# A two-model forward pass on one core: 512-column split products issued as two 256-column halves

## The chip, the cores and the metric

The kernel runs on one core of a Trainium2 chip. The metric is the device time of one execution in microseconds; the time given for a kernel is the median of its runs. TensorE does the matrix products, VectorE (DVE in the profile), ScalarE (ACT) and GpSimd (POOL) the rest, and SyncE (SP) issues the transfers.

## The reference, cut to what matters

Two small models run one after the other on 256 tokens of width 1024, all in float32. The first has a retention layer, a per-layer embedding, a layer of native sparse attention (NSA) and a second per-layer embedding. The second puts 16 meta tokens ahead of the 256, mixes a gated delta rule with forgetting attention, and ends with a SwiGLU block of width 2816. Nearly all of the arithmetic is in products of the token rows with weight matrices:

```
proj = rmsnorm(h, g_norm) @ w_in                # retention: 1024 x 6144
y = (silu(gate) * o) @ w_out                    # retention: 2048 x 1024
gate = sigmoid(rmsnorm(h, g) @ w_gate)          # embedding, twice: 1024 x 1024
proj = rmsnorm(h, g_kv) @ w_kv                  # 1024 x 3072
proj = rmsnorm(h, g_norm) @ w_in                # NSA: 1024 x 4144
y = (silu(gate) * o) @ w_out                    # NSA: 2048 x 1024
proj = u @ w_in[l]; ... @ w_out[l]              # second model: 1024 x 3600, 1024 x 1024
h = h + (silu(x @ w_gate) * (x @ w_up)) @ w_down  # 1024 x 2816 twice, 2816 x 1024
```

## The kernel before

**Split products.** A float32 product is made of three one-pass products. Each operand is kept as a high part (its value rounded to the one-pass type `F32R`) and a low part (what the rounding left). `parts3` (line 762) adds high by high, low by high and high by low into one PSUM region; the low by low term is left out. ScalarE rounds a weight (line 1621, `high_parts<-ring`), VectorE subtracts (line 2060, `ring_parts<-ring,high_parts`), each in halves of 1024 columns.

**Units.** The weights come in units of 128 x 2048 numbers (1 MB each) through a ring of four buffers `ring`; the high parts go to three buffers `high`. SyncE issues a unit when TensorE has begun the unit three before it and so has left the one in that buffer (`units_used`, which the first matmul of a unit raises). The splitting engines run a fixed number of units ahead of TensorE. A matmul's wait for its unit is on `units_low`.

**Two shapes of product.** Units of kind A hold 8 tiles (contraction) by 256 output channels; there the weight tile of 128 x 128 is the stationary operand and the 256 tokens (272 in the second model) are the moving one, so a pass has 256 or 272 columns (`project_a`, line 803 on; `project_a_pair`; `channels_input`). Units of kind B hold 4 tiles by 512 channels; there the 128 x 128 tile of tokens is stationary and the weights move, so a pass has 512 columns and fills a PSUM bank. All the products of 512 columns are of kind B, and their functions are `project_b` (line 818 on), `retention_output` (1006), `first_rows_output` (1216), `mix_output` (1411), `rows_input` (1447) and the down projection (1597 and 1603). A unit of kind B gives 8 split products, 24 matmuls; a unit of kind A gives 16, 48 matmuls. The compression layer of NSA (`first_layer`) has products of its own, not through `parts3`: the stationary operand is a 128 x 124 tile that holds both parts, the moving one 256 columns of a weight unit.

**The 488 products of 512 columns, in order of time**: retention values and gate (`rv`, `rg`, 128 products), retention output (`ro`, 64), first embedding gate (`pg`, 32), the row half of the shared key and value projection (`kvB`, 32), NSA output (`no`, 64), second embedding gate (`pg`, 32), the `gz` gate rows (16) and the mixer output (`mo`, 32), the down projection (`dn`, 88). Three passes each make 1464 matmuls. From the second embedding to `mo`, the token tiles stand in rows of 272 with an offset of 16; elsewhere they stand in rows of 256.

**Order.** Each engine has its own instruction list, written out by hand in the order of the network; between projections TensorE transposes token tiles (`turn`, line 841), does the attention products and the delta rule. `narrow` (line 757) is a list of small products that `parts3` puts between its passes; it is filled only ahead of products of 256 columns (`nq`, `ng`) and is used up by them.

Of the kernel before, what the change touches and what calls it, by code (L numbers as in the profile page):

```python
# [351 lines left out]
def two_models_kernel(nc, x, meta, weights, side, params, tabs, ret_tabs, p_t, gains, out):  # L352
    ctx = ExitStack()
    with ctx:
# [10 lines left out]
        def as_r(ap):  # L365

            return bass.AP(tensor=one_pass[ap.tensor.name], offset=ap.offset, ap=ap.ap)
# [303 lines left out]
        def odd_blocks(ap, lv):  # L671

            return ap.rearrange("p (b two m) -> p b two m", two=2, m=LEVELS[lv])[:, :, 1, :]

        def level_rows(lv, c):
            return chunk_part(c, G1, 1024, 1) if lv else z_rows(c)
# [79 lines left out]
        def _(pe):  # L756
            narrow = []

            def mm(out, lhsT, rhs, first, last):
                return pe.matmul(out, lhsT, rhs, start=first, stop=last, skip_group_check=True)  # L760

            def parts3(product, out, lhsT, rhs, first, last):

                product(out, as_r(lhsT[0]), as_r(rhs[0]), first, False)
                if narrow:
                    narrow.pop(0)()
                product(out, as_r(lhsT[1]), as_r(rhs[0]), False, False)
                if narrow:
                    narrow.pop(0)()
                return product(out, as_r(lhsT[0]), as_r(rhs[1]), False, last)  # L770

            def next_unit(k):

                u = begun[0]
                begun[0] += 1
                if u == 0:
                    pass
                elif IS_SPLIT[u]:
                    pe.wait_ge(sem("units_low"), 2 * SPLITS[u] - 1)
                else:  # L780
                    pe.wait_ge(sem(f"unit_in{u % RING}"), 16 * (u // RING + 1))
                first = [u > 0]

                def product(*args):
                    ins = mm(*args)
                    if first[0]:
                        ins.then_inc(sem("units_used"), 1)
                    first[0] = False
                    return ins

                low = ring[:, u % RING * UNIT:(u % RING + 1) * UNIT].rearrange("p (k c) -> p k c", k=k)
                hi = high[:, u % HIGH * UNIT:(u % HIGH + 1) * UNIT].rearrange("p (k c) -> p k c", k=k)
                second = [u > 0 and IS_SPLIT[u]]

                def w(i, c):
                    if second[0] and 2 * i >= k:
                        pe.wait_ge(sem("units_low"), 2 * SPLITS[u])
                        second[0] = False
                    return hi[:, i, c], low[:, i, c]

                return w, product

            def project_a(keys, src, c0, n):

                w, product = next_unit(KD)
                for f in range(2):
                    key = keys[f * (len(keys) - 1)]
                    base = f * n if len(keys) == 1 else 0
                    if f == 0 or len(keys) == 2:
                        bank = main.open(pe, key)  # L810
                    for k in range(KD):
                        x_k = src(k, c0, n)
                        ins = parts3(product, bank[:, base:base + n], w(k, slice(f * P, (f + 1) * P)), x_k,
                                     k == 0, k == KD - 1)
                    if f == 1 or len(keys) == 2:
                        main.full(ins, key)

            def project_b(keys, src, rows, kt, ready=None, started=None):

                banks = [main.at(key) if started and n == 0 else main.open(pe, key) for n, key in enumerate(keys)]  # L820
                for k0 in range(0, kt, 4):
                    if ready:
                        ready(k0)
                    w, product = started if started and k0 == 0 else next_unit(4)
                    for n, bank in enumerate(banks):
                        if started and k0 + n == 0:
                            continue
                        c0, m = rows[n]
                        for k in range(4):
                            x_k = src(k0 + k, c0, m)  # L830
                            ins = parts3(product, bank[0:m, :], x_k, w(k, slice(0, 512)), k0 + k == 0,
                                         k0 + k == kt - 1)
                        if k0 + 4 == kt:
                            main.full(ins, keys[n])
# [69 lines left out]
            def x_src(k, c0, n):  # L904
                tile_ready("x", k)
                return kt_cols(xT, k, c0, n), kt_cols(xT2, k, c0, n)

            def tokens_src(k, c0, n):
                tile_ready("x", k)
                return kt_cols(xT, k, c0, n, T), kt_cols(xT2, k, c0, n, T)  # L910
# [24 lines left out]
            w, product = next_unit(KD)  # L935
            for f in range(4):
                pe.wait_ge(sem(piece_low(f)), 1)
                for half in range(2):
                    for k in (2 * f, 2 * f + 1):
                        ins = parts3(product, bank[:, half * T:(half + 1) * T], w(k, slice(half * P, (half + 1) * P)),  # L940
                                     tokens_src(k, 0, T), half == 0 and k == 0, k == KD - 1)
# [8 lines left out]
            for kt in range(KD):  # L950
                ins = pe.transpose(bank[:, kt * M:(kt + 1) * M], R[0:M, R3 + kt * P:R3 + (kt + 1) * P], ident[0:M, 0:M])
# [3 lines left out]
            def qk_tile(which, hd, half, c0, n):  # L955
                return kt_cols(R, which * 8 + hd * 2 + half, c0, n, T, R1)

            pe.wait_ge(sem("rotated"), 8)
            for hd in range(RH):
# [3 lines left out]
                for half in range(2):  # L963
                    ins = mm(bank[:, T:T + P], qk_tile(1, hd, half, P, P), qk_tile(0, hd, half, P, P),
                             half == 0, half == 1)
# [284 lines left out]
            for k in range(KD):  # L1250
                w_k = gates_high[:, k * 16:(k + 1) * 16], side_sb[:, SIDE_G2 + k * 16:SIDE_G2 + (k + 1) * 16]
                ins = parts3(mm, bank[0:16, 0:TM], w_k, x_src(k, 0, TM), k == 0, k == KD - 1)
# [7 lines left out]
            def mat(buf, base, c, hd):  # L1260
                n = CHUNKS[c][1]
                return buf[0:n, base + C_OFF[c] + hd * n:base + C_OFF[c] + (hd + 1) * n]

            def of_head(rows, c, hd):
                n = CHUNKS[c][1]
                return rows[:, hd * n:(hd + 1) * n]

            def chunk_rows(base, c, hd):

                buf, b0 = base  # L1270
                return buf[0:CHUNKS[c][1], b0 + c * 512 + hd * P:b0 + c * 512 + (hd + 1) * P]
# [180 lines left out]
            for kind, *key in mixer_order():  # L1452
# [35 lines left out]
                elif kind == "Lz":  # L1488
                    lv, c = key
# [9 lines left out]
                    for hd in range(GH):  # L1499
                        ins = mm(bank[0:n, hd * n // 2:(hd + 1) * n // 2].rearrange("p (b m) -> p b m", m=LEVELS[lv]),  # L1500
                                 of_head(level_rows(lv, c), c, hd), odd_blocks(mat(PTb, C_ALL, c, hd), lv), True, True)
                    aux.full(ins, ("z", lv, c))
                    if lv > 1:
                        bank = aux.open(pe, ("x", lv, c))
                        for hd in range(GH):
                            ins = pe.transpose(bank[0:n, hd * n:(hd + 1) * n], mat(PTb, C_ALL, c, hd), ident[0:n, 0:n])  # L1506
                        aux.full(ins, ("x", lv, c))
                elif kind == "Lx":
                    lv, c = key
# [6 lines left out]
                    for hd in range(GH):  # L1516
                        half = slice(hd * n // 2, (hd + 1) * n // 2)
                        ins = mm(bank[0:n, half], mat(PTb, 0, c, hd), z[:, half], True, True)
                    aux.full(ins, ("y", lv, c))
                elif kind == "W":  # L1520
                    c = key[0]
# [3 lines left out]
                    for hd in range(GH):  # L1525
                        ins = mm(bank[:, hd * P:(hd + 1) * P], chunk_rows(RK, c, hd), mat(PTb, C_ALL, c, hd), True, True)
                    aux.full(ins, ("gw", c))
                elif kind == "Vn":
                    c = key[0]
# [8 lines left out]
                    for hd in range(GH):  # L1538
                        o = bank[0:n, hd * P:(hd + 1) * P]
                        ins = mm(o, mat(PTb, C_ALL, c, hd), chunk_rows(RV, c, hd), True, c == 0)  # L1540
                        if c:
                            w0 = (c - 1) * 512 + hd * P
                            ins = mm(o, nw[:, w0:w0 + P], R[:, state + hd * P:state + (hd + 1) * P], False, True)
                    aux.full(ins, ("vn", c))
                else:
                    c = key[0]
                    t0, n = CHUNKS[c]
                    wait_read(pe, aux, ("vn", c))
                    if c:
                        pe.wait_ge(sem("q_scaled"), c)  # L1550
                        bank = aux.open(pe, ("go", c))
                        for hd in range(GH):
# [3 lines left out]
                            ins = mm(o, R[:, k0:k0 + P], R[:, v_new + hd * P:v_new + (hd + 1) * P], False, True)  # L1556
                        aux.full(ins, ("go", c))
                    if c < 2:
                        wait_read(pe, aux, ("kt", c))
                        bank = aux.open(pe, ("st", c))  # L1560
                        for hd in range(GH):
                            ins = mm(bank[:, hd * P:(hd + 1) * P], chunk_rows(KDEC, c, hd),
                                     R[0:n, v_new + hd * P:v_new + (hd + 1) * P], True, True)
# [19 lines left out]
            def hidden_src(k, t):  # L1583
                return tuple(hidden(k, part)[:, t * P:(t + 1) * P] for part in range(2))

            banks = {}
            for c in range(2):
                for k0 in range(0, 20, 4):
# [3 lines left out]
                    w, product = next_unit(4)  # L1592
# [6 lines left out]
            w, product = next_unit(2)  # L1599
            for t in range(TT):  # L1600
                for c in range(2):
                    for k in range(2):
                        ins = parts3(product, banks[c, t], hidden_src(20 + k, t), w(k, slice(c * 512, (c + 1) * 512)),
                                     False, k == 1)
# [1258 lines left out]
```

## Time and profile before

| | |
|---|---|
| median of 3 runs | 957.28 us (954.9 to 960.26) |
| the profiled execution: its time, its span | 956.0 us, 954.2 us |
| TensorE matmul busy | 941.8 us, 99% of the span, 6366 matmuls |
| TensorE weight loads busy | 843.8 us, 88%, 6366 loads |
| VectorE, ScalarE, GpSimd busy | 66%, 50%, 13% |
| granted TensorE clock | 0.999 of full speed |
| weight transfers | 135 of 1024 KB, mean 158 GB/s in all |

Matmuls overlap in the pipe: a record of a 512-column pass is about 0.39 us long, but the next pass starts about 0.23 us after it. So the busy time of TensorE says only that it was never without work; how fast it works is read from the distance between the starts of successive matmuls, called the pitch here. A window of the trace gives the number of matmuls in it and with that the pitch. The window counts each matmul that overlaps it, also those that started before it and were still in the pipe: 0.28 us of 256-column records, or 0.39 us of 512-column records.

### The profile page before, as it was taken

The page shows a single profiled execution, that of the slowest core. Times are in us where ns is not written, and L with a number is a line of the kernel's source. Part 1 is how long each engine was busy: PE and PEld are TensorE (multiplying, and loading weights), DVE is VectorE, ACT ScalarE, POOL GpSimd, SP SyncE. Part 2 cuts the span into 40 slices and gives each one's busy share as a digit, 9 for nine tenths or more (in the row PEclk, how much of TensorE's full clock was granted, in tenths as well). Part 3 has the DMA queues.
Part 4 walks back from the last instruction along what each step waited for, and adds up shares of the span by engine and source line. Part 5 has one row for each costly group of instructions (what it writes and reads, how often), then busy time and mean ns, then how long its engine had stood idle before and what let it go on. Part 6 is the DMA issues. An engine that isn't in the chain of part 4 may idle for free.

```text
span 954.2 us, 15895 instructions
## 1 busy us (share of the span) xinstructions
PE 941.8 (99%) x6366; PEld 843.8 (88%) x6366; DVE 632.9 (66%) x930; ACT 478.9 (50%) x843; POOL 122.0 (13%) x128
## 2 busy tenths in 40 slices
PE   9999999999999999999999999999999999999997
PEld 8988778878998999998888789999998899999885
DVE  5974467557884766678874477988554677676543
ACT  6334446455654554466653566664335554444432
POOL 1000032000320000101410004212320111111001
PEclk9999999999999999999999999999999999999999
DMA  8735445555555763332025553522101455565551
GB/s 327 291 138 180 158 147 177 177 177 177 177 194 214 289 231 133 131 136 89 1 88 178 175 177 134 177 89 89 46 1 45 167 190 196 184 213 179 191 206 45
DMA packets 23516, 150.55 MB, mean 158 GB/s; under 512 B 3564, under 2 KB 3848, under 8 KB 6168
## 3 DMA queue, kind: packets, MB, share of 16 engines
q1 hardware_dynamic: 23104, 149.39, 44.8%
q8 instruction: 51, 0.84, 0.3%
q10 hardware_dynamic: 344, 0.18, 0.1%
q14 instruction: 17, 0.14, 0.1%
HBM read 148.50 MB, written 1.05 MB: 157 GB/s over the span
## 4 chain that ended last, share of the span: by engine, by line
PE 86%; DVE 7%; ACT 3%; issue 1%; DMA 1%; POOL 0%; SPq 0%; ACTq 0%; POOLq 0%; DVEq 0%
PE psum L760 83%; DVE ring_parts L2060 3%; PE psum L841 1%; DVE R L2385 1%; ACT high_parts L1621 1%; ACT R L1806 1%; PE psum L1174 1%; DMA h<-in_x 1%; DMA ring<-in_weights 1%; DVE R L2337 1%; PE psum L1506 1%; DVE PTb_parts L2356 0%; ACT tmp L1659 0%; ACT R L1628 0%; PE psum L1357 0%
## 5 line engine op out<-in xcount | busy, mean ns | idle before, releaser
L2060 DVE TENSOR_TENSOR ring_parts<-ring,high_parts 128x1024 fp32r<-128x1024 f32 (+1 forms) x272 | 333.3, 1264 | 146.7 <-ACT high_parts L1621 145.3
L1621 ACT CAST high_parts<-ring 128x1024 fp32r<-128x1024 f32 x268 | 268.2, 1050 | 187.0 <-PE psum L760 149.2
L760 PE MATMUL psum<-xT_parts,high_parts 128*128 128x256 f32 (+1 forms) x1024 | 227.5, 284 | 1.5 <-issue 0.6
L760 PE MATMUL psum<-xT_parts,ring_parts 128*128 128x256 f32 (+1 forms) x704 | 200.1, 284 | 0.0
L760 PEld LDWEIGHTS psum<-xT_parts,high_parts 128*128 128x128 f32 x1024 | 172.3, 188 | 3.0 <-issue 1.2
L760 PE MATMUL psum<-high_parts,R_parts 128*128 128x512 f32 (+1 forms) x528 | 164.9, 386 | 0.0
L760 PE MATMUL psum<-R_parts,high_parts 128*128 128x256 f32 x832 | 156.0, 277 | 0.0
L760 PE MATMUL psum<-high_parts,xT_parts 128*128 128x512 f32 x480 | 154.2, 397 | 0.0
L760 PEld LDWEIGHTS psum<-xT_parts,ring_parts 128*128 128x128 f32 x704 | 132.9, 189 | 0.1
L760 PEld LDWEIGHTS psum<-R_parts,high_parts 128*128 128x128 f32 x832 | 130.5, 188 | 0.1
L760 PEld LDWEIGHTS psum<-high_parts,R_parts 128*128 128x128 f32 (+1 forms) x528 | 98.7, 188 | 20.5
L760 PEld LDWEIGHTS psum<-high_parts,xT_parts 128*128 128x128 f32 x480 | 89.4, 188 | 20.9 <-issue 1.9
L760 PE MATMUL psum<-ring_parts,xT_parts 128*128 128x512 f32 x256 | 100.6, 393 | 0.0
L760 PE MATMUL psum<-ring_parts,R_parts 128*128 128x512 f32 (+1 forms) x264 | 99.3, 381 | 0.0
L760 PE MATMUL psum<-R_parts,ring_parts 128*128 128x256 f32 x352 | 97.2, 276 | 0.0
L760 PE MATMUL psum<-PTb_parts,high_parts 128*128 128x256 f32 x256 | 73.8, 288 | 0.0
L760 PEld LDWEIGHTS psum<-R_parts,ring_parts 128*128 128x128 f32 x352 | 66.1, 188 | 0.0
L760 PEld LDWEIGHTS psum<-ring_parts,R_parts 128*128 128x128 f32 (+1 forms) x264 | 49.6, 188 | 9.6
L760 PEld LDWEIGHTS psum<-ring_parts,xT_parts 128*128 128x128 f32 x256 | 48.1, 188 | 10.6
L760 PEld LDWEIGHTS psum<-PTb_parts,high_parts 128*128 128x128 f32 x256 | 48.2, 188 | 0.0
L760 PE MATMUL psum<-R 128*128 128x128 f32 (+3 forms) x248 | 47.1, 324 | 0.6 <-DVE R_parts L2572 0.6
L2737 POOL TENSOR_TENSOR R<-R,small 128x1024 f32<-128x1024 f32 x12 | 22.8, 1899 | 194.7 <-DVE small L2332 194.7
(354 smaller groups left out, 1144.4 us busy)
## 6 DMA issues: line engine op xcount, KB each, us to landing
ring<-in_weights SPq DMA_DIRECT2D x135, 1024.0 KB, 4.9
h<-in_x SPq DMA_DIRECT2D x4, 256.0 KB, 4.6
ring<-in_weights SPq DMA_DIRECT2D x4, 256.0 KB, 6.2
ring<-in_weights SPq DMA_DIRECT2D x2, 512.0 KB, 7.6
G<-in_gains SPq DMA_DIRECT2D x2, 512.0 KB, 7.7
out<-xn SPq DMA_DIRECT2D x2, 512.0 KB, 2.6
R<-in_ret_tabs SPq DMA_DIRECT2D x1, 768.0 KB, 13.6
tab<-in_tabs SPq DMA_DIRECT2D x1, 663.5 KB, 5.9
```

Source lines behind the costliest of these rows:

```text
L760: return pe.matmul(out, lhsT, rhs, start=first, stop=last, skip_group_check=True)
L841: ins = pe.transpose(bank[:, k * T + t * P:k * T + (t + 1) * P], src(2 * f + k, t), ident)
L1174: ins = pe.transpose(bank[:, n * P:(n + 1) * P], R[:, c0:c0 + P], ident)
L1506: ins = pe.transpose(bank[0:n, hd * n:(hd + 1) * n], mat(PTb, C_ALL, c, hd), ident[0:n, 0:n])
L1621: act.copy(as_r(hi), value).then_inc(sem("units_high"), 1)
L1806: ins = act.activation(R[:, c0:c0 + n_keys], bank[:, n * n_keys:(n + 1) * n_keys], ACT.Exp, bias=nmx[:, col:col + 1], accum_out=esum[:, co ...
L2060: return dve.tensor_tensor(as_r(value), value, value_of(hi), ALU.subtract)
L2337: main.free(dve.tensor_tensor(two(R[:, R4 + n * 512:R4 + (n + 1) * 512]), two(bank), token_scale2, ALU.mult), key)
L2385: ins = dve.scalar_tensor_tensor(y, raw[:, j, k:k + TM], param("conv_w_2", 12 * k + j), y, ALU.mult, ALU.add)
L2737: pool.tensor_tensor(p, p, spread(esc[:, i * 8:i * 8 + 2 * nh], 1024 // (2 * nh)), ALU.mult).then_inc(sem("nsa_p"), 1)
```

## The change

In `parts3`, a product whose output is two-dimensional and 512 columns wide is no longer three passes of 512 columns. It is three passes over the left 256 columns of the bank, then three over the right 256, in the order high by high, low by high, high by low, with the same stationary tiles. Only the first pass of the left half carries the start flag of the bank. Outputs of other widths, and the three-dimensional output of the NSA values (line 1199), go the old way. The new branch doesn't call `narrow`.

```
             def parts3(product, out, lhsT, rhs, first, last):
 
+                if len(out.shape) == 2 and out.shape[1] == 512:
+                    for c in (slice(0, 256), slice(256, 512)):
+                        product(out[:, c], as_r(lhsT[0]), as_r(rhs[0][:, c]), first and c.start == 0, False)
+                        product(out[:, c], as_r(lhsT[1]), as_r(rhs[0][:, c]), False, False)
+                        ins = product(out[:, c], as_r(lhsT[0]), as_r(rhs[1][:, c]), False, last)
+                    return ins
                 product(out, as_r(lhsT[0]), as_r(rhs[0]), first, False)
```

## Rows read from the trace of the kernel before

**Rows 1.** The page: busy time and instructions of each engine, and their chain.
```profile
PE 941.8 (99%) x6366; PEld 843.8 (88%) x6366; DVE 632.9 (66%) x930; ACT 478.9 (50%) x843; POOL 122.0 (13%) x128
...
PE 86%; DVE 7%; ACT 3%; issue 1%; DMA 1%; POOL 0%; SPq 0%; ACTq 0%; POOLq 0%; DVEq 0%
```
**Rows 2.** Groups: out<-moving,stationary, shapes, count, busy us, mean ns, idle before.
```profile
L760 PE MATMUL psum<-high_parts,R_parts 128*128 128x512 f32 x496 | 157.2, 393 | 0.0
L760 PE MATMUL psum<-high_parts,xT_parts 128*128 128x512 f32 x480 | 154.2, 397 | 0.0
L760 PE MATMUL psum<-ring_parts,xT_parts 128*128 128x512 f32 x256 | 100.6, 393 | 0.0
L760 PE MATMUL psum<-ring_parts,R_parts 128*128 128x512 f32 x232 | 91.5, 394 | 0.0
...
L760 PEld LDWEIGHTS psum<-R_parts,high_parts 128*128 128x128 f32 x832 | 130.5, 188 | 0.1
L760 PEld LDWEIGHTS psum<-high_parts,R_parts 128*128 128x128 f32 x496 | 92.8, 188 | 20.5
```
**Rows 3.** Windows of 512-column passes: stretch; length, PE and PEld busy (count), clock.
```profile
284.00:304.00 20.00, 20.00 (x89) 16.43 (x88) 1.00 0.59 206
...
493.50:533.00 39.50, 39.50 (x171) 32.01 (x171) 1.00 0.51 171
548.00:560.00 12.00, 12.00 (x53) 9.76 (x52) 1.00 0.57 199
...
888.00:946.00 58.00, 58.00 (x255) 47.61 (x254) 1.00 0.42 145
```
**Rows 4.** Windows of passes of 256 columns, the same columns.
```profile
24.00:51.00 27.00, 27.00 (x232) 27.00 (x231) 1.00 0.73 261
...
250.00:282.00 32.00, 32.00 (x285) 32.00 (x284) 1.00 0.64 224
...
314.00:319.00 5.00, 5.00 (x45) 5.00 (x44) 1.00 0.92 382
...
362.00:364.00 2.00, 2.00 (x19) 2.00 (x18) 1.00 0.91 360
404.00:409.00 5.00, 5.00 (x46) 5.00 (x45) 1.00 0.52 170
...
435.00:440.00 5.00, 5.00 (x47) 5.00 (x46) 1.00 0.57 192
...
609.00:612.00 3.00, 3.00 (x28) 3.00 (x27) 1.00 0.62 164
...
778.00:886.00 108.00, 108.00 (x955) 108.00 (x954) 1.00 0.58 202
```
**Rows 5.** Timeline of the NSA values and first NSA output products.
```profile
489.29 0.28 PE L760 MATMUL psum<-PTb_parts,R_parts 128*128 128x256 f32 x1
...
490.37 0.28 PE L760 MATMUL psum<-PTb_parts,R_parts 128*128 128x256 f32 x1
490.49 0.63 PE L760 MATMUL psum<-high_parts,R_parts 128*128 128x512 f32 x2
490.96 0.40 PE L760 MATMUL psum<-ring_parts,R_parts 128*128 128x512 f32 x1
491.19 0.63 PE L760 MATMUL psum<-high_parts,R_parts 128*128 128x512 f32 x2
```
**Rows 6.** Timeline of the compression layer, first and last of 16 passes.
```profile
360.02 0.28 PE L760 MATMUL psum<-high_parts,xn_parts 128*124 128x256 f32 x1
...
361.90 0.28 PE L760 MATMUL psum<-xT_parts,high_parts 128*128 128x256 f32 x1
```
**Rows 7.** The chain in order of time: eight transposes of 128 columns.
```profile
231.77 0.87 PE psum L841 x8
```
**Rows 8.** The page's groups: the two engines that split the weights.
```profile
L2060 DVE TENSOR_TENSOR ring_parts<-ring,high_parts 128x1024 fp32r<-128x1024 f32 (+1 forms) x272 | 333.3, 1264 | 146.7 <-ACT high_parts L1621 145.3
L1621 ACT CAST high_parts<-ring 128x1024 fp32r<-128x1024 f32 x268 | 268.2, 1050 | 187.0 <-PE psum L760 149.2
```
**Rows 9.** TensorE's waits for the split: us in total, times, longest.
```profile
PE psum L760 <- DVE ring_parts L2060: 0.5, 2, 0.3
```

## The prediction, made before the changed kernel ran

> **What bounds the kernel now.** I read the page first, for who is busy and who ends the chain, then the groups with their shapes kept apart, then windows of single stretches, and last the timeline where a window was too coarse. The page [rows 1] is to show that TensorE is never without work: 99% busy, and 86% of the chain that ends last. Whatever changes the number of nanoseconds that a matmul takes from the stream changes the end of the kernel by the same amount, as long as nothing else becomes the bound. The groups [rows 2] are to show two things. The four groups of 512 columns hold 496 + 480 + 256 + 232 = 1464 passes, which is 3 for each of 488 products, so all of them can be costed. And none of them stood idle before, so in these stages TensorE waits for nothing: neither for a weight unit nor for a bank.
>
> The mean of 393 to 397 ns in those groups is the length of a record in the pipe, not what a pass costs. The cost is the pitch, from windows. A window counts the passes that overlap it; for 512 columns that is 0.39 / 0.23 = 1.7 passes too many, for 256 columns 0.28 / 0.115 = 2.4.
>
> 512 columns [rows 3]: 20 / (89 - 1.7) = 229.1 ns, 58 / (255 - 1.7) = 229.0; in the NSA output 39.5 / (171 - 1.7) = 233.3; with token rows of 272, 12 / (53 - 1.7) = 233.9, where one pass more or less in the count is 2% (so I take 232).
>
> 256 columns [rows 4]: 32 / (285 - 2.4) = 113.2 ns and 108 / (955 - 2.4) = 113.4; but 27 / (232 - 2.4) = 117.6, 5 / (45 - 2.4) = 117.4 and 3 / (28 - 2.4) = 117.2. A third level is in the timeline of the NSA values [rows 5]: nine passes from 489.29 to 490.37, 120.0 ns each; the 512-column product that follows takes 490.49 to 491.19, 233.3 ns a pass.
>
> So the same instruction runs at two or three levels: 113.3 (call it the even level), 117.7, and 120. The stretch at 24 us and the one at 778 us are the same kind of stream, a weight tile stationary and 256 tokens moving; I found nothing in the shapes that sets the level. It seems to be taken at the start of a stretch and kept. That is what this forecast hangs on, because 2 x 113.3 = 226.7 is less than 229.0, and 2 x 117.7 = 235.4 and 2 x 120 = 240 are more.
>
> **The change, part by part.**
>
> Removed: 1464 passes of 512 columns. Today they cost, by product of three: 344 products in rows of 256 at 3 x 229.0 = 687.0 ns; 64 of the NSA output at 3 x 233.3 = 700 ns; 80 in rows of 272 (second embedding gate 32, gz 16, mixer output 32) at 3 x 232 = 696 ns. The sum is 236.3 + 44.8 + 55.7 = 336.8 us, or 690.2 ns a product.
>
> Added: 2928 passes of 256 columns, each with its load of a 128 x 128 stationary tile; the third and the fourth pass load the same tile, and it is loaded twice (in the compression layer [rows 6] two passes in a row have the same tile and still take 1.88 us / 16 = 117.5 ns each). The trace has no pass of exactly this kind: 128 token columns stationary, 256 columns of a weight unit moving. The nearest rows bound it. Below: 113.3 ns, the even level [rows 4], made of the same column counts with the operands exchanged. Above: 120 ns [rows 5], tokens moving and V stationary, the slowest steady stream of this shape. Between them lies the compression layer [rows 6], nearest in its moving operand (the same buffers, 256 columns), 117.5 ns with an odd tile of 124 columns. A product becomes 6 x 113.3 = 680, 6 x 117.7 = 706 or 6 x 120 = 720 ns.
>
> Which value I take, by stage. For the 344 products: of the streams of 256 columns with rows of 256, those at 117.6 or so last 34 us (up to 55 us) and some 20 us in short pieces ([rows 4] has two), while the even ones last from 250 to 283, 778 to 887 and, in pieces, most of 394 to 443 (5 / (46 - 2.4) = 114.7 and 5 / (47 - 2.4) = 112.1 in two of them), so about a fifth of the passes are slow. 0.8 x 680 + 0.2 x 706 = 685 ns, against 687: 344 x -2 = -0.7 us. For the NSA output, the NSA values before it feed it at 120 and today's 512-column passes there keep their extra 6.7 ns each [rows 3, 5]: 720 against 700, 64 x 20 = +1.3 us. For rows of 272, tiles at odd offsets gave 117.2 [rows 4] and 117.5 [rows 6]; 6 x 117.5 = 705 against 696, 80 x 9 = +0.7 us. Sum: +1.3 us.
>
> The bounds of the sum: all at 113.3, 488 x 680 = 331.8 us, -5.0 us; all at 117.7, 344.5 us, +7.7 us; all at 120, 351.4 us, +14.6 us.
>
> The Trainium skill ("TensorE: Matmul & The Clock Gate", section "Back-to-back issue gap") states a fixed part of 2.5 ns in each warm matmul beside its columns, which speaks against halving: 3 more passes are 7.5 ns a product, an estimate of +3.7 us. The rows agree in part: they show no fixed part at all at the even level (113.3 against half of 226 to 229), and a larger one, 5 to 7 ns, at the other two.
>
> What doesn't cost. The order left, then right only moves when the first half is done; the bank is handed over after the last pass as before. The `narrow` list is empty in all 512-column products. The unit's first matmul still raises the signal for the next transfer. Issue: streams of 256 columns already bring a load and a matmul every 113 ns for 108 us on end [rows 4]. Splitting: a kind-B unit lasts 8 x 687 = 5.5 us today and 5.4 to 5.8 us after, while the split takes 2 x 1.26 us of VectorE and 2 x 1.05 us of ScalarE [rows 8]; TensorE waited for it 0.5 us in all [rows 9], and kind-A units of 48 x 113.3 = 5.4 us are fed by the same split. If that cover were gone, a unit would wait as in the chain's 7% of VectorE [rows 1], which lies outside these stages. The four-deep ring sees no other pace.
>
> So nearly nothing is gained or lost: the profiled execution of 956.0 us (span 954.2 and 1.8 around it) goes to 957.3; against the median of 957.28, 1.3 us above that profile, I say 958.6.
>
> **The rivals.**
>
> The slow level everywhere. Each stage starts after transposes or scores and could take 117.7, or 120, and keep it. For it: the slow level followed directly on small products at 24 us, and the nearest moving operand shows 117.5. Against it: four fifths of the passes of 256 columns escape it. Its price is +7.7 us, 965.0; with 120 everywhere 971.9. It decides against the kernel beyond the measurement once the mean pitch of the new passes is over (690.2 + 4.8 / 0.488) / 6 = 116.7 ns. Chance 0.2 for a mean of 116.7 to 118.5, 0.06 for more.
>
> The even level everywhere: the halving evens out the odd nanoseconds of the 512-column passes, NSA output included. For it: after 512-column passes at 229 the 256-column streams at 250 and 778 us settled at 113.3. Against it: rows of 272 never show it. -5.0 us, 952.3. Chance 0.1 for a gain of over 2.5 us.
>
> The load becomes the pace. In 512-column streams the load unit is busy 16.43 of 20 us, in 256-column streams all the time [rows 3, 4], and eight transposes of 128 columns, take 0.87 / 8 = 109 ns each [rows 7], although they have half the columns: if that is the load, it has some 4 ns to spare in a pitch of 113.3. Here the tile loaded comes from the token buffers and twice as often; were it to take 125 ns, a product would be 750 ns and the time 957.28 + 488 x 0.060 = 986. For it: the busy column. Against it: the loads of token tiles under 512-column passes have the same record, 188 ns, as those of weight tiles under 256-column passes, which do keep up [rows 2, 4]. Chance 0.04.
>
> The same section of the Trainium skill gives about 131 ns as the sustained spacing at 512 columns and 81 at 128, by which small passes would be much dearer than half; no row shows such a spacing, the 512-column passes stand at 229.
>
> **How the numbers follow.** 0.6 for the forecast case (-2.5 to +4.5 us: 954.8 to 961.8), 0.1 for the even level, 0.2 and 0.06 for the slow ones, 0.04 for the load. About 0.5%, 4.8 us, is what a measurement of this kernel can tell from no change. The even level reaches 952.5 only in full, so faster gets 0.06, slower 0.28 (0.2 + 0.06, half of the load's chance taken as smaller than its price), same 0.66. The range goes from 953.5, with some of the even level, to 966, which takes in the slow level.
>
> **What would show it.** The page should have 7830 matmuls and as many loads, TensorE 99% busy, the load unit over 95%. Windows in the down projection should hold 113.3 ns a pass (0.6 us less for the whole of it), the NSA output 118 to 120, the second embedding gate 117 to 118. If the first windows of `rv` and `rg` show 117.7, the slow rival is right; a load record longer than 188 ns [rows 2] and a pitch over 120 shows the load. New idle time of TensorE before a 512-column bank's product, with VectorE's split as releaser, would refute the cover.

## The result and the profile after

The changed kernel takes 969.54 us (4 runs, 967.63 to 972.85) against 956.09 us (4 runs, 954.56 to 960.26) of the kernel before: ratio 1.0134, 95% interval 1.0104 to 1.0164. It is slower by 1.3%, where 958.6 us and no measurable change had been forecast. The interval leaves out 1, and both sets of runs stand apart: the fastest of the changed kernel is 7.4 us above the slowest of the kernel before.

The page of the changed kernel, busy time and instructions of each engine, then the chain; they answer to [rows 1].

```profile
PE 956.2 (98%) x7830; PEld 920.6 (95%) x7830; DVE 635.0 (65%) x930; ACT 479.2 (49%) x843; POOL 120.5 (12%) x128
...
PE 87%; DVE 7%; ACT 3%; issue 1%; DMA 1%; POOL 0%; SPq 0%; ACTq 0%; POOLq 0%; DVEq 0%
```

The counts are as forecast, and TensorE is as busy and holds as much of the chain as before. Two waits of TensorE are longer than in the first trace of the kernel before, and neither is the change's: at the start, ahead of anything that was changed, it waits 3.5 us in all for the transfer of the tokens (`h<-in_x`) instead of 0.8, and once 1.4 us for VectorE in the second model. The second trace of the kernel before has 2.0 us and 1.4 us for the same two. What changed is the pitch. Windows of the changed kernel (stretch; length, PE busy and count, PEld busy and count, granted clock), which answer to [rows 3] and [rows 4]:

```profile
24.00:51.00 27.00, 27.00 (x241) 27.00 (x240) 1.00 0.74 278
74.00:104.00 30.00, 30.00 (x257) 30.00 (x256) 1.00 0.55 190
114.00:130.00 16.00, 16.00 (x143) 16.00 (x142) 1.00 0.54 193
180.00:205.00 25.00, 25.00 (x215) 25.00 (x214) 1.00 0.47 173
256.00:282.00 26.00, 26.00 (x223) 26.00 (x222) 1.00 0.56 201
...
500.00:538.00 38.00, 38.00 (x325) 38.00 (x324) 1.00 0.52 182
...
640.00:670.00 30.00, 28.55 (x206) 27.09 (x206) 0.83 0.16 53
...
790.00:890.00 100.00, 100.00 (x851) 100.00 (x850) 1.00 0.54 194
908.00:962.00 54.00, 54.00 (x461) 54.00 (x460) 1.00 0.39 137
```

With 2.4 overlapping passes taken off each count, the halves in `rv` (74 to 104) stand at 30 / 254.6 = 117.8 ns, in `ro` (180 to 205) at 117.6, in `no` (500 to 538) at 117.8, in the down projection (908 to 962) at 54 / 458.6 = 117.7; only those of the first `rg` (114 to 130) are near the even level, 113.8. More telling are the streams that the change doesn't touch. The SwiGLU gate and up stream (790 to 890), even at 113.4 before, now takes 100 / 848.6 = 117.8. The key and value stream at 256 went from 113.2 to 117.9. The first stream of all (24 to 51) went the other way, from 117.6 to 113.2, although no instruction ahead of it differs between the two kernels.

The starts of the same matmuls in the two traces, in us:

| stretch | before | after | added |
|---|---|---|---|
| start of the span to 20.9 | 0 to 20.93 | 0 to 22.82 | +1.9 |
| first stream, untouched | 20.93 to 55.42 | 22.82 to 56.04 | -1.3 |
| `rv`, `rg`, `ro`, first `pg`, halves | 55.42 to 237.98 | 56.04 to 241.70 | +3.1 |
| kvA, untouched | 237.98 to 283.08 | 241.70 to 287.96 | +1.2 |
| kvB, halves | 283.08 to 305.06 | 287.96 to 310.57 | +0.6 |
| compression, queries, scores, untouched | 305.06 to 493.44 | 310.57 to 497.86 | -1.1 |
| `no`, second `pg`, halves | 493.44 to 567.17 | 497.86 to 572.43 | +0.8 |
| second model up to the mixer's end, with `gz` | 567.17 to 740.01 | 572.43 to 750.67 | +5.4 |
| `mo`, halves | 740.01 to 765.80 | 750.67 to 776.97 | +0.5 |
| SwiGLU gate and up, untouched | 765.80 to 887.03 | 776.97 to 902.38 | +4.2 |
| down projection, halves | 887.03 to the end | 902.38 to the end | +1.7 |

The halves added 6.8 us in this trace (a little more with the 16 `gz` products, which lie in the row of the second model), and the SwiGLU stream 4.2. The -1.3 of the first stream can't be the change's, since it runs ahead of the first changed instruction. The +1.2 of kvA is not in every execution: matched in the same way, the second trace of the changed kernel (below) has 0.0 for the first stream, +0.1 for kvA, +7.3 for the halves and again +4.2 for SwiGLU. So what the change did to a stream that it doesn't touch, in both traces, is the 4.2 us of SwiGLU.

The 5.4 us in the second model are nearly all TensorE's clock: the window from 640 to 670 has a granted clock of 0.83, which is about 10 us at the lower level of 1.2 GHz; the engine was busy 28.55 of 30 us there, between streams, with many small products. The four executions of the changed kernel differ in it: two took 967.6 and 967.8 us and two 971.2 and 972.9, and the clock over the span was 0.996 and 0.999 in the first two, 0.994 and 0.993 in the others. It is no effect of the change: a second trace of the kernel before (below) has such a dip at 638 us, the kernel with halves in the down projection only (below), whose instructions are those of the kernel before up to 887 us, has two, at 635 and 652 us, and of 66 later executions of the kernel before 29 had a clock of 0.994 or less. The difference is there without the dips: the changed kernel's execution at 0.999 took 967.8 us, and the 23 of the kernel before at 0.999 took 953.7 to 957.2. The two faster ones are 11.6 and 11.8 us above the profiled execution of the kernel before; the table without its row of 5.4 gives 11.6.

### The profile page after: what moved, and what is told of

Read it like the earlier page. It is cut to its first block, busy times and chain, and to the rows that moved or that the text cites. A ratio compares the mean times of both kernels' runs of the same rounds, so it can differ in the third digit from the quotient of the medians.

```text
span 971.2 us, 18823 instructions
## 1 busy us (share of the span) xinstructions
PE 956.2 (98%) x7830; PEld 920.6 (95%) x7830; DVE 635.0 (65%) x930; ACT 479.2 (49%) x843; POOL 120.5 (12%) x128
## 4 chain that ended last, share of the span: by engine, by line
PE 87%; DVE 7%; ACT 3%; issue 1%; DMA 1%; POOL 0%; SPq 0%; ACTq 0%; POOLq 0%; DVEq 0%
PE psum L760 84%; DVE ring_parts L2066 3%; PE psum L847 1%; DVE R L2391 1%; ACT R L1812 1%; DMA h<-in_x 1%; PE psum L1180 1%; ACT high_parts L1627 1%; DVE R L2343 1%; PE psum L1512 0%; DVE PTb_parts L2362 0%; ACT tmp L1665 0%; ACT R L1634 0%; PE psum L1363 0%; DVE PTb L2538 0%
## 5 line engine op out<-in xcount | busy, mean ns | idle before, releaser
L760 PE MATMUL psum<-high_parts,R_parts 128*128 128x256 f32 (+1 forms) x1024 | 190.1, 280 | 0.0
L760 PE MATMUL psum<-high_parts,xT_parts 128*128 128x256 f32 x960 | 178.3, 282 | 0.0
L760 PE MATMUL psum<-R_parts,high_parts 128*128 128x256 f32 x832 | 160.6, 281 | 0.0
L760 PEld LDWEIGHTS psum<-high_parts,R_parts 128*128 128x128 f32 (+1 forms) x1024 | 159.6, 187 | 0.0
L760 PEld LDWEIGHTS psum<-high_parts,xT_parts 128*128 128x128 f32 x960 | 148.7, 188 | 2.1 <-issue 1.9
L760 PE MATMUL psum<-ring_parts,xT_parts 128*128 128x256 f32 x512 | 142.8, 279 | 0.0
L760 PE MATMUL psum<-ring_parts,R_parts 128*128 128x256 f32 (+1 forms) x496 | 137.3, 279 | 0.0
L760 PEld LDWEIGHTS psum<-ring_parts,xT_parts 128*128 128x128 f32 x512 | 96.2, 188 | 0.0
L760 PEld LDWEIGHTS psum<-ring_parts,R_parts 128*128 128x128 f32 (+1 forms) x496 | 93.1, 188 | 0.0
```

## The experiments

All of them are told by the level of the streams, 113.3 (even) or 117.8 (slow) for 256 columns, 229.0 or 233.3 for 512.

**The two kernels again.** No edit.

> The kernel before, unchanged, for a second trace. Theory P (the level of a stream, 113.3 or 117.8 ns a pass, is fixed by the program: by the instructions ahead of it): the same streams are even and slow as in the first trace, 24 to 51 us slow, 250 to 282 and 778 to 886 even, and the time is 954 to 958. Rival R (the level is drawn anew in each execution): at least one of these three streams stands at the other level, and the SwiGLU stream alone moves the time by 954 x 4.4 ns = 4.2 us when it does.

959.52 us. Windows, which answer to [rows 4] at 24, 250 and 778 us:

```profile
26.00:53.00 27.00, 27.00 (x232) 27.00 (x231) 1.00 0.72 267
250.00:282.00 32.00, 32.00 (x285) 32.00 (x284) 1.00 0.58 201
790.00:880.00 90.00, 90.00 (x797) 90.00 (x796) 1.00 0.57 197
```

The same counts as in the first trace: slow, even, even (90 / 794.6 = 113.3). Every long stream of the second trace stands at the level that it had in the first, as theory P has it. Two traces are few, though. The kernel with halves in the down projection only (below) has the same instructions up to 887 us, and in its trace the first stream came out even. Its window, to be compared with the first one above:

```profile
26.00:53.00 27.00, 27.00 (x241) 1.00 0.78 278
```

> The changed kernel, unchanged, for a second trace. Theory P: the first stream (25 to 53 us) even, the streams of rv, rg 0, ro, kvA and kvB, no, the SwiGLU gate and up products and dn slow at 117.8, as in the first trace; 967 to 969 without, up to 973 with a stretch of TensorE at 1.2 GHz. Rival R: the list of slow streams differs from the first trace's, and the time lies anywhere from 957 to 969. If the two stretches at 1.2 GHz around 643 and 656 us are the change's own, they are there again; if they are chance, they aren't.

972.74 us, windows of the second trace of the changed kernel:

```profile
24.00:51.00 27.00, 27.00 (x232) 27.00 (x231) 1.00 0.72 274
114.00:130.00 16.00, 16.00 (x139) 16.00 (x137) 1.00 0.52 193
256.00:282.00 26.00, 26.00 (x232) 26.00 (x231) 1.00 0.62 229
790.00:890.00 100.00, 100.00 (x851) 100.00 (x850) 1.00 0.55 194
```

The first three stand at the other level than in the first trace (117.6, 117.1, 113.2), the SwiGLU stream at the same one. So neither theory is right alone. From about 380 us on, every long stream has the same level in all traces of the same code (a short one in the mixer output has not). Up to there it can differ from one execution to the next, with whole passes too: over the 14 traces of this document, whose code is the same up to the first stream, that stream is even in 6 and slow in 8. In the 12 traces without added bf16 products, kvA is even in all 6 that have whole passes ahead of it; in the 6 with halves it is slow in 3, those in which the first stream is even, and even in the other 3. In those 6, `rg` has the level of the first stream.

The dips of the clock at 643 and 656 us are there again, but that doesn't make them the change's: the traces of this document have from none to three dips ahead of the last few us of the span, with and without halves.

**Halves in the down projection only.** The condition of the change gets a switch that is set ahead of the last loop:

```
-                if len(out.shape) == 2 and out.shape[1] == 512:
+                if halved[0] and len(out.shape) == 2 and out.shape[1] == 512:
...
+            halved[0] = True
             banks = {}
             for c in range(2):
```

> Only the 88 products of the down projection are made in halves; all ahead of them is as before. Theory P: the SwiGLU stream ahead is even as before, and the down projection follows it without a break and stays even: 6 x 113.3 = 680 ns a product against 687, -0.6 us in all, so 955.5 against 956.1. Rival T (a pass with tokens stationary and 256 columns of weights moving always stands at 117.8): 706 to 707 ns a product, +1.75 us, with the stream ahead still even.

955.38 us against 958.06 of the kernel before, ratio 0.998 (0.9954 to 1.0006). Windows of the SwiGLU stream and of the down projection in halves:

```profile
790.00:880.00 90.00, 90.00 (x797) 1.00 0.57 191
895.00:945.00 50.00, 50.00 (x444) 1.00 0.43 148
```

50 / 441.6 = 113.2 ns a pass, against 117.7 for the same 528 matmuls in the changed kernel. Rival T falls: tokens stationary and 256 weight columns moving can run at the even level, and a product then costs 680 ns, not 687. The gain of 0.6 us is less than the measurement can tell.

**Another order of the six passes.**

```
-                    for c in (slice(0, 256), slice(256, 512)):
-                        product(out[:, c], as_r(lhsT[0]), as_r(rhs[0][:, c]), first and c.start == 0, False)
-                        product(out[:, c], as_r(lhsT[1]), as_r(rhs[0][:, c]), False, False)
-                        ins = product(out[:, c], as_r(lhsT[0]), as_r(rhs[1][:, c]), False, last)
+                    halves = (slice(0, 256), slice(256, 512))
+                    for c in halves:
+                        product(out[:, c], as_r(lhsT[0]), as_r(rhs[0][:, c]), first and c.start == 0, False)
+                    for c in halves:
+                        product(out[:, c], as_r(lhsT[1]), as_r(rhs[0][:, c]), False, False)
+                    for c in halves:
+                        ins = product(out[:, c], as_r(lhsT[0]), as_r(rhs[1][:, c]), False, last)
```

> As the change, but the six passes go by stationary tile: high by high left and right, low by high left and right, high by low left and right. Theory P: the levels are those that the entries into the streams give, and each is 113.3 or 117.8 as in the changed kernel, 965 to 970. Rival O (the slow level comes from the order of the change, three accumulations in a row on one half with the tile changing at every pass): with the tile the same in every second pass the streams of halves stand at 113.3, and the time falls to 957 to 962, the untouched SwiGLU stream slow or not.

971.83 us, ratio 1.0141 (1.0103 to 1.0178). Windows:

```profile
74.00:104.00 30.00, 30.00 (x257) 1.00 0.54 196
...
790.00:890.00 100.00, 100.00 (x851) 1.00 0.55 195
908.00:962.00 54.00, 54.00 (x461) 1.00 0.39 137
```

In these windows the counts are to the pass those of the changed kernel. The order within a product didn't matter, and the same tile twice in a row didn't help. Rival O falls.

**Disturbing a running stream.** A bank that nobody reads takes small extra products between the gate and the up half of each n:

```
             for n in range(1, 11):
                 project_a([("fg", n)], ffn_src, 0, T)
+                between(plan.get(n))
                 project_a([("fu", n)], ffn_src, 0, T)
```

> The changed kernel with small extra products, whose results nobody reads, put into the SwiGLU gate and up stream, one kind between the gate and up halves of each n: two f32 products of 128 columns with a broadcast tile (as spread_roots has them) at n = 1, 8 and 9, one such at 2, one F32R pass of 256 columns at 3, eight transposes at 4, one transpose at 5, one bf16 product at 6, one F32R pass of 128 columns at 7. In the traces so far each spread_roots turned a slow stream into an even one or the reverse. Theory F (f32 products flip the level): slow at 117.8 up to n = 1, even at 113.3 until the next f32 product; the three pairs each flip it. Rival S (the level belongs to the program around it and not to the last disturbance): 117.8 throughout.

Windows between the disturbances, first of the changed kernel with them (970.47 us):

```profile
784.00:790.00 6.00, 6.00 (x53) 1.00 0.93 332
792.00:802.00 10.00, 10.00 (x90) 1.00 0.59 212
804.00:813.00 9.00, 9.00 (x81) 1.00 0.64 233
815.00:824.00 9.00, 9.00 (x79) 1.00 0.64 233
827.00:836.00 9.00, 9.00 (x78) 1.00 0.66 223
839.00:847.00 8.00, 8.00 (x70) 1.00 0.60 220
850.00:859.00 9.00, 9.00 (x82) 1.00 0.64 233
861.00:870.00 9.00, 9.00 (x79) 1.00 0.64 228
873.00:882.00 9.00, 9.00 (x82) 1.00 0.68 235
884.00:895.00 11.00, 11.00 (x96) 1.00 0.53 192
```

In 9 us, 82 (81) passes are the even level and 79 (78) the slow one. In order: slow; after the pair of f32 products (n = 1) even; after one f32 product even; after one odd F32R pass of 256 columns slow; after eight transposes slow; after one transpose slow; after the bf16 product even; after the F32R pass of 128 columns slow; after the pair even; after the pair slow.

> The same extra products in the kernel before. Theory F: even at 113.3 up to n = 1, slow at 117.8 from there until the next flip, so at each place the opposite level of the run on the changed kernel, or the same wherever the kind of disturbance sets a level rather than flips it. Rival S: 113.3 throughout.

Windows of the kernel before (967.04 us) ahead of the first pair and behind it, and around the last four disturbances:

```profile
780.00:787.00 7.00, 7.00 (x64) 1.00 0.83 300
789.00:798.00 9.00, 9.00 (x79) 1.00 0.67 231
...
847.00:856.00 9.00, 9.00 (x82) 1.00 0.69 235
858.00:867.00 9.00, 9.00 (x79) 1.00 0.69 231
869.00:879.00 10.00, 10.00 (x90) 1.00 0.61 211
881.00:890.00 9.00, 9.00 (x79) 1.00 0.68 231
```

At all the places in order: even, then slow after the pair, and slow after the single f32 product, the odd pass, the eight transposes and the one; even after the bf16 product, slow after the F32R pass of 128 columns, even after the pair, slow after the pair. Rival S falls in both: the level belongs to the last disturbance and what it met. The pair flipped the level at all six places in the two kernels. The single f32 product did not: it left even even and slow slow, so theory F holds for the pair alone.

Both kernels have this pair of their own (`spread_roots`) ahead of the first stream, in kvA and in the SwiGLU stream. Taking the mean distance of the 12 passes ahead of it and behind it, it flipped the level at 48 of 50 places in all the traces, at all 28 in kvA and SwiGLU; the two exceptions are ahead of the first stream. This shows where the two kernels part. The 46 SwiGLU passes just ahead of that pair stand at 117.8 ns in the kernel before and at 113.4 in the changed one, and the pair turns the first into even and the second into slow. The pair is the same; what the change moved is the level that it meets.

The timeline of the pair of n = 8 in the changed kernel shows how short it is (an f32 product has two records):

```profile
871.04 0.28 PE L761 MATMUL psum<-R_parts,high_parts 128*128 128x256 f32 x1
871.16 0.61 PE L761 MATMUL psum<-tab,small 128*128 128x128 f32 x4
871.52 0.37 PE L761 MATMUL psum<-R_parts,high_parts 128*128 128x256 f32 x1
871.73 0.28 PE L761 MATMUL psum<-R_parts,ring_parts 128*128 128x256 f32 x1
```

**One flip, timed.** Only the pair at n = 1 is kept.

> The changed kernel with one extra pair of f32 products of 128 columns in the SwiGLU stream, after the gate half of n = 1; nothing else. It adds two products (0.4 us). Theory F: the 1414 passes behind it, those of the gate and up stream and of the down projection in halves, go from 117.8 to 113.3 ns: -6.4 us + 0.4, so about 962 against about 968 for the changed kernel, and 1.005 to 1.009 of the kernel before. Rival S: +0.4 us, about 1.014.

962.97 us against 957.35, ratio 1.006 (1.004 to 1.008). Windows behind the pair, in the SwiGLU stream and in the down projection:

```profile
792.00:880.00 88.00, 88.00 (x779) 1.00 0.55 196
900.00:950.00 50.00, 50.00 (x443) 1.00 0.41 146
```

88 / 776.6 = 113.3 and 50 / 440.6 = 113.5: work was added, and the changed kernel lost more than half of what it had cost, as theory F has it.

> The kernel before with the same extra pair. Theory F: 886 passes of 256 columns go from 113.3 to 117.8 ns, +4.0 us, and the 264 of 512 columns behind them may go from 229.0 to 233.3, +1.1 us; with the pair's 0.4 the ratio is 1.004 to 1.006. Rival S: +0.4 us, 1.000.

961.67 us, ratio 1.0059 (1.0037 to 1.0082). The same stretches in the kernel before with the pair; the second is of 512 columns and answers to the last window of [rows 3]:

```profile
790.00:880.00 90.00, 90.00 (x766) 1.00 0.55 188
900.00:950.00 50.00, 50.00 (x216) 1.00 0.41 145
```

90 / 763.6 = 117.9 and 50 / 214.3 = 233.3. The kernel before, with nothing added but two products of 0.4 us and the bank that takes them, is slower by 0.6%. This also completes the down projection's table: 512 columns at 229.0 and 233.3, halves at 113.2 and 117.7, the same operands in all four. A product costs 687 or 700 whole, 680 or 706 in halves.

**Which halves turn the SwiGLU stream.** The switch is on in `mix_output` alone, or off there alone.

```
+                    halved[0] = True      # False in the other
                     ins = parts3(product, bank, mix_src(4 * half + k, *rows[t]), w(k, slice(0, 512)),
                                  half == 1 and k == 0, half == 0 and k == 3)
+                    halved[0] = False     # True in the other
```

> Only the 32 products of the mixer output, the last 512-column products ahead of the SwiGLU stream, are made in halves. Theory H (the halves change the level at which the following stream is entered): as in the changed kernel, the gate and up stream is slow after its last interruption: 984 passes x 4.4 ns = 4.3 us, the down projection in 512 columns at 233.3 instead of 229.0, 1.2 us, and the 32 products themselves +0.3 us; ratio 1.005 to 1.007. Rival N (only the products made in halves get dearer): +0.3 us, ratio 1.000.

964.61 us against 957.67, ratio 1.0078 (1.0053 to 1.0103), for 32 products in halves. Its windows:

```profile
790.00:890.00 100.00, 100.00 (x852) 1.00 0.54 186
900.00:950.00 50.00, 50.00 (x216) 1.00 0.43 147
```

100 / 849.6 = 117.7 and 233.3, in code that is the same as before instruction for instruction.

> Halves everywhere but in the mixer output. Theory H: the SwiGLU stream is entered as in the kernel before and runs even, and the down projection in halves with it: 1510 passes x 4.4 ns = 6.7 us and 0.3 less than the changed kernel; ratio about 1.006. Rival N: 0.3 us less than the changed kernel, ratio 1.013.

963.45 us, ratio 1.0059 (1.0033 to 1.0085), with 456 of the 488 products in halves:

```profile
790.00:890.00 100.00, 100.00 (x885) 1.00 0.55 199
900.00:950.00 50.00, 50.00 (x444) 1.00 0.43 154
```

100 / 882.6 = 113.3 and 113.2. Theory H holds in both: 32 products in halves cost as much as 456, because of where they stand. Which of the two costs more is not shown, as the intervals overlap.

**Trying to set the level everywhere.** A bf16 product of 128 columns, overwritten by the start of the bank that it goes to, ahead of the second token tile of each row projection and at three other places:

```
+            def bf16_product(bank, tile):
+                x = as_r(tile).bitcast(BF16)[:, 0:P]
+                mm(bank[:, 0:P], x, x, True, True)
...
+                        if k0 == 0 and n == 1:
+                            bf16_product(bank, src(k0, c0, m)[0])
```

> The changed kernel with one bf16 product of 128 columns, whose result is overwritten, ahead of the second token tile's products of every row projection, of the retention output, of kvA 2 and of the SwiGLU gate 1. In both runs with disturbances such a product was followed by the even level where the level before was slow. Theory E (the halves are dear only because of the level at which a stream happens to run, whatever the stream): the streams of rv, rg, ro, pg and kvB go to 113.3, 680 ns a product; each bf16 product costs 0.13 us, 14 of them 1.8 us; some 3000 passes x 4.4 ns = 13 us less than the changed kernel, so 955 to 958 against about 969, ratio 0.996 to 1.002. Rival V (the level of the row projections in halves is their own, 117.8 whatever the entry): SwiGLU, dn and kvA alone profit, 1800 x 4.4 = 8 us, ratio 1.006 to 1.008. Rival W (a bf16 product flips and does not set): streams that were even turn slow, and the ratio is over 1.008.

966.58 us against 958.67 (ratio 1.0084, 1.0056 to 1.0112); the profiled execution was the fastest, 959.97, the others 964.7 to 968.3. Its windows:

```profile
74.00:97.00 23.00, 23.00 (x198) 1.00 0.51 184
114.00:124.00 10.00, 10.00 (x87) 1.00 0.50 164
126.00:133.00 7.00, 7.00 (x64) 1.00 0.49 183
...
180.00:208.00 28.00, 28.00 (x249) 1.00 0.54 190
790.00:890.00 100.00, 100.00 (x885) 1.00 0.55 196
```

117.6, 118.2, 113.6, 113.5, 113.3. In `rg` and `ro` the same kind of product stood at both levels within one trace and mostly changed at the bf16 product: it flips there and doesn't set, as W says, though SwiGLU came out even. By the time alone V and W can't be told apart, since the interval takes in the ratios of both; V falls by `rg` and `ro`. The streams of `rv` and of the first `pg` stayed slow through it. The time is not what E wanted, so these products don't get rid of the slow level. The windows show the fastest of six executions; its clock was 0.999 and that of the others 0.992 to 0.996, which explains a part of their extra time, and their levels weren't seen.

> The kernel before with the same bf16 products. Theory E: the streams of 512 columns stand at 229.0 already and can gain only in the NSA output (233.3, 180 passes, 0.8 us); the extra products cost 1.8 us; ratio 1.001 to 1.003, and of the two kernels with bf16 products the one with halves is the faster, by up to 488 x 7 ns = 3.4 us. Rival V: the one with halves is slower by 5 us or more. Rival W: the SwiGLU stream, even today, turns slow, +4 to 5 us more, ratio 1.006 to 1.009.

958.6 us, ratio 1.0019 (0.9994 to 1.0043). Windows of the 512-column passes in `rv` and `no` (the latter answers to the second of [rows 3]):

```profile
85.00:95.00 10.00, 10.00 (x45) 1.00 0.54 185
494.00:534.00 40.00, 40.00 (x177) 1.00 0.53 182
```

10 / 43.3 = 231 within the coarseness of one pass in 45, and 40 / 175.3 = 228.2: `no` went from 233.3 to about 229, and in the retention the 512-column passes kept 229 over every bf16 product of that trace. The same disturbances that move halves between 113.4 and 118 in `rg` and `ro` left whole passes there alone. So no version measured here beats the kernel before beyond the interval; the nearest is the down projection alone in halves, 0.998.

## Why the prediction was wrong

**What bounds the kernel** was right: TensorE holds 87% of the chain, and the nanoseconds of its passes went into the end one by one, but for 1.1 us. Between 329 and 341 us the kernel before waits for a weight transfer and its split (TensorE is busy 15.22 of the 16 us from 330 to 346), and 1.1 of the 5.5 us by which the changed kernel was late there vanished in that wait (0.9 of 5.3 in its second trace).

**The cost of a product in halves, by level** was right: 6 x 113.3 = 680 and 6 x 117.7 = 706 ns were measured, and 120 came nowhere in a stream of halves; the NSA output, forecast at 720 ns a product, stood at 706 too. With rows of 272 it was 118.1 ns a pass in the second embedding gate (709 ns a product, forecast 705).

The Trainium skill ("TensorE: Matmul & The Clock Gate", section "Back-to-back issue gap") has a fixed 2.5 ns in each warm matmul, by which six passes for three would be 7.5 ns dearer, an estimate. The measurement differs at the even level, where a product got cheaper, 680 against 687 ns; at the slow level, 706 against 700, it comes near.

The load unit was busy all the time, as the load's rival had it, and was not the pace by itself, since halves reached 113.2.

**The step that failed is "Which value I take, by stage".** It took the share of slow passes in the streams of before, a fifth, for the share in the new ones, +1.3 us in sum. That share said nothing of the new streams: `rv`, `ro`, `no`, `mo` and the down projection were slow in both traces of the changed kernel, `rg` in one of them, and the cost of the halves was +6.8 and +7.3 us, close to the bound "all at 117.7" of +7.7 us. The slow rival named this with a chance of 0.2. Why the halves enter nearly all their streams slow stays open.

**The second failure is what was left out of the sum.** The prediction had it that a level "seems to be taken at the start of a stretch and kept", and still costed 2928 passes only. If the level depends on how a stream is entered, then a change ahead of an untouched stream can move that stream. It did, with +4.2 us in the SwiGLU stream in both traces; kvA moved by +1.2 us in one of them only. Forcing it both ways showed it: 32 halved products ahead of SwiGLU cost 0.8%, and two added products brought the ratio from 1.013 to 1.006. No rival had this term; with it the slow rival would have been 965.0 + 4.2 = 969.2. That this lies so near to the measured 969.54 is partly luck, since two of the four executions hold some 5 us of the clock's dips.

**The cover** held: TensorE waited 0.3 us in all for the split of the weights (0.5 before), and the chain shows no new wait for a bank or a weight unit.

**What stays open.** What in the engine makes the two levels, and why an entry takes the one or the other. That a short interruption flips it was shown, and for the pair of f32 products it came close to a rule (48 of 50). For the other kinds no rule was found: the SwiGLU stream was even behind the bf16 product in all four traces that have it, slow before it in three and already even in the fourth, while in other streams the same product flipped either level or left it alone. So which level a program meets at an entry can be read from a trace, but not foretold. That whole passes in the retention kept 229 over every interruption that was tried, while in `no` and the down projection they are found at 229 and at 233, was seen and not explained. The clock's dips were not explained either.

## What to carry to other kernels

Halving a pass doesn't save or cost a fixed amount: here it was -1% of the product at the even level, +1% at the slow one, and +3% where the halves were slow and the whole passes weren't, which was the usual case. When a change shifts the time by about a per cent in a kernel that TensorE bounds, compare the pitch in the streams that were not changed before explaining the one that was; the matmul counts of equal windows give it. Include a stream ahead of the change: the first one here moved by 1.3 us without any cause in the edit, and only a second trace tells such a move from an effect. A forecast for such a kernel needs a term for streams downstream flipping, which here is 4.4 ns a pass, up to 7 us for the last 1500 passes.

## What the runs showed of the hardware

One stream of F32R passes, with the same operands and the same instructions, runs at one of two steady paces and keeps it for over 1500 passes and 170 us: 113.3 or 117.8 ns at 256 columns, 229.0 or 233.3 at 512, at a granted clock of 1.00 in all these windows. Two f32 products of 128 columns with nothing else between (0.36 us in the timeline above) flipped it at all six places in the disturbed runs, and at 48 of 50 places of all 14 traces. From about 380 us on, the long streams had the same level in every trace of the same code; the first stream, at 21 us, was even in 6 and slow in 8 traces of the same code, and kvA in the kernels with halves was slow in 3 of 6. A short stretch is an exception: the first 34 passes of the mixer output stood at 233.3 ns in the trace with halves in the down projection only, and at 228.9 in the five other traces with only whole passes up to there.
